# Layer 0's q, k and v: the weight columns split at k-tile 4 in place of 8, and both parts begun k-tile by k-tile in eight banks

## The reference, cut to what matters

```python
def hybrid_layer(x, c_act, g, w_ada, b_ada, w_in, w_out, dec_f, dec_b):
    mod = c_act @ w_ada + b_ada
    shift, scale, gate = jnp.split(mod, 3, axis=-1)
    h = rms_norm(x, g) * (1.0 + scale[:, None]) + shift[:, None]
    proj = jnp.einsum('bsd,df->bsf', h, w_in)
    q_a, k_a, v_a, z_a, q_r, k_r, v_r, z_r = jnp.split(proj, IN_SPLIT_IDX, axis=-1)
    ...
    y_a = dilated_attention_mixture(q_a, k_a, v_a)
    y_r = bidirectional_retention(q_r, k_r, v_r, dec_f, dec_b)
    y = jnp.concatenate([y_a * jax.nn.silu(z_a), y_r * jax.nn.silu(z_r)], axis=-1)
    return x + gate[:, None] * jnp.einsum('bsf,fd->bsd', y, w_out)
```

## Time and profile before

| | |
|---|---|
| median of 3 runs (range) | 1496.59 us (1496.10 to 1496.89) |
| profiled execution, its time | 1496.42 us |
| its span in the profile | 1494.6 us |
| mean granted TensorE clock | 0.992 |
| busy | PE 1427.5 us (96%), DVE 1169.1 (78%), ACT 722.5 (48%), POOL 117.9 (8%) |
| DMA | 448.85 MB, mean 300 GB/s |
| chain that ended last | PE 76%, DVE 14%, issue, ACT and DMA 3% each |

### The profile page before, as it was taken

How to read it: one execution, slowest core, us unless ns; L and a number is a source line. 1 busy time by engine, 2 the same in 40 slices (tenths; PEclk the granted TensorE clock), 3 DMA queues, 4 the chain that set the end, 5 groups by cost and what they waited for, 6 DMA issues and landing times.

```text
span 1494.6 us, 19097 instructions
## 1 busy us (share of the span) xinstructions
PE 1427.5 (96%) x6634; PEld 1177.8 (79%) x6634; DVE 1169.1 (78%) x1458; ACT 722.5 (48%) x1034; POOL 117.9 (8%) x217
## 2 busy tenths in 40 slices
PE   4799999999999899999999999989999999999996
PEld 3677777887887688888887878878888888888885
DVE  5999898877999799898667659878697865556566
ACT  4464554554434634444556644464345544455431
POOL 1111001001000001010010100000010000000000
PEclk9999999999999999999999999999999999999998
DMA  9999999877999599999867679759698786555762
GB/s 389 414 412 413 392 359 394 287 264 244 385 416 347 191 407 383 412 384 381 309 214 252 188 269 364 262 192 356 244 385 300 252 282 207 178 179 155 266 194 89
DMA packets 99870, 448.85 MB, mean 300 GB/s; under 512 B 11424, under 2 KB 13776, under 8 KB 76496
## 3 DMA queue, kind: packets, MB, share of 16 engines
q1 hardware_dynamic: 69840, 249.33, 46.9%
q0 software_dynamic: 26352, 185.63, 31.8%
q10 hardware_dynamic: 3600, 12.85, 2.2%
HBM read 445.65 MB, written 2.12 MB: 300 GB/s over the span
## 4 chain that ended last, share of the span: by engine, by line
PE 76%; DVE 14%; issue 3%; ACT 3%; DMA 3%; SPq 0%; POOL 0%; DVEq 0%; ACTq 0%
PE bank L741 22%; PE bank L743 22%; PE bank L742 22%; DVE gw L1425 6%; DVE w_lo L1417 4%; PE bank L951 2%; PE bank L899 2%; DMA gw<-in_t_ada 1%; PE bank L716 1%; PE bank L908 1%; DMA raw<-in_t_steps 1%; DVE area L1425 1%; ACT probs L1081 1%; PE bank L927 1%; PE bank L881 1%
## 5 line engine op out<-in xcount | busy, mean ns | idle before, releaser
L1022 ACT CAST w_hi<-raw 128x1024 fp32r<-128x1024 f32 x448 | 468.7, 1050 | 647.5 <-PE bank L743 544.4
L1405 DVE TENSOR_TENSOR w_lo<-raw,w_hi 128x1024 fp32r<-128x1024 f32 x372 | 451.4, 1223 | 260.4 <-ACT w_hi L1022 259.5
L741 PE MATMUL bank<-w_hi,act_hi 128*128 128x512 f32 x1504 | 601.3, 400 | 3.1 <-DVE w_lo L1405 3.1
L742 PE MATMUL bank<-w_lo,act_hi 128*128 128x512 f32 x1536 | 598.7, 390 | 0.0
L743 PE MATMUL bank<-w_hi,act_lo 128*128 128x512 f32 x1504 | 587.5, 391 | 0.0
L1425 DVE CUSTOM_DVE_ANT_0 gw<-gw,c_act 128x2048 f32<-128x2048 f32 x170 | 388.1, 2285 | 4.0 <-DMA gw<-in_t_ada 4.0
L742 PEld LDWEIGHTS bank<-w_lo,act_hi 128*128 128x128 f32 x1536 | 289.1, 188 | 57.2
L741 PEld LDWEIGHTS bank<-w_hi,act_hi 128*128 128x128 f32 x1504 | 282.9, 188 | 61.0 <-issue 3.6
L743 PEld LDWEIGHTS bank<-w_hi,act_lo 128*128 128x128 f32 x1504 | 282.6, 188 | 60.7
L1417 DVE TENSOR_TENSOR w_lo<-raw,w_hi 128x1024 fp32r<-128x1024 f32 x84 | 101.6, 1220 | 15.3 <-ACT w_hi L1022 15.1
L585 POOL DMA_DIRECT2D gw<-in_t_mod x96 | 51.6, 537 | 729.3 <-DVE products L1425 723.1
(11 more groups left out here) (174 smaller groups left out, 1003.3 us busy)
## 6 DMA issues: line engine op xcount, KB each, us to landing
raw<-in_t_steps SPq DMA_DIRECT2D x464, 512.0 KB, 5.7
gw<-in_t_mod POOLq DMA_DIRECT2D x96, 1024.0 KB, 7.7
gw<-in_t_ada POOLq DMA_DIRECT2D x42, 1024.0 KB, 8.3
gw<-in_t_kv_mod POOLq DMA_DIRECT2D x32, 1024.0 KB, 8.0
area<-in_t_ada POOLq DMA_DIRECT2D x6, 1024.0 KB, 10.7
area<-gate_rows ACTq DMA_DIRECT2D x3, 1024.0 KB, 12.9
area<-in_ln_g ACTq DMA_DIRECT2D x2, 1024.0 KB, 6.1
area<-in_ln_b ACTq DMA_DIRECT2D x2, 1024.0 KB, 9.2
```

The source lines that it names most:

```text
L741: nc.tensor.matmul(dst, hi, w[:, k], start=(kt == 0), stop=False)
L742: nc.tensor.matmul(dst, hi, w_lo[:, j % SLOTS, k], start=False, stop=False)
L1022: nc.scalar.copy(w_hi[:, b], raw[:, j % SLOTS]).then_inc(hi_ready, 1)
L1405: nc.vector.tensor_tensor(w_lo[:, j % SLOTS], raw[:, j % SLOTS], w_hi[:, j % LEAD].bitcast(F32), ALU.subtract).then_inc(lo_ready, 1)
```

## The change

The boundary between the two parts goes from k-tile 8 to k-tile 4 (`FIRST_KT`). Steps 0 to 7 are the eight-bank part for k-tiles 0 to 3 with chunks 0 and 2, then 3 and 4. Steps 8 to 19 give chunks 5, 8, 9, 6, 7, 1 the same four k-tiles, two steps each. Steps 20 to 43 are a second eight-bank part: k-tiles 4 to 15 one after the other for chunks 0 and 2 (banks 4 to 7) and 6 and 7 (banks 0 to 3), with the order of the two turned round at k-tile 15. Steps 44 to 79 give chunks 4, 1, 3, 5, 8, 9 the twelve k-tiles, six steps each. Rows of `w_ada` are worked one k-tile per three steps for k-tiles 4 to 7, then one per two and a half (`ROWS_AT`), the last at the same step as before. The five places for rows serve rows 0 to 9 and no longer 0 to 14. SP holds the loads to four ahead of DVE up to step 19 in place of 15. The three rows of pair 2 start at place 12 in place of 9. The small loads and the two bias tables go from behind steps 32 to 45 to behind 44 to 57, the decays, lambda and the decay tables with them by seven or eight steps. Numbers of steps, matmuls, splits and additions are the same, and the layout of the weights on the host follows the order.

```diff
-DECAYS_AT, LAMBDA_AT, C_AT = (3, 1), (3, 4), (4, 9)
-DECAY_TABLE_AT = {(3, 6): 0, (3, 8): 1, (3, 10): 2, (3, 12): 3}
+DECAYS_AT, LAMBDA_AT, C_AT = (3, 9), (3, 11), (4, 9)
+DECAY_TABLE_AT = {(3, 13): 0, (3, 15): 1, (4, 1): 2, (4, 4): 3}
...
-FIRST_ORDER = (4, 5, 8, 9, 6, 7)
-SECOND_ORDER = (6, 7, 0, 2, 4, 1, 3, 5, 8, 9)
+FIRST_KT = 4
+FIRST_WIDE = ((0, 2), (3, 4))
+FIRST_ORDER = (5, 8, 9, 6, 7, 1)
+SECOND_WIDE = ((0, 2), (6, 7))
+SECOND_ORDER = (4, 1, 3, 5, 8, 9)
+FIRST_SHORT, SECOND_SHORT = FIRST_KT // STEP_KT, (KT - FIRST_KT) // STEP_KT
+SECOND_AT = HEAD_STEPS + FIRST_SHORT * len(FIRST_ORDER)
+SHORT_AT = SECOND_AT + 2 * (KT - FIRST_KT)
+ROWS_AT = {kt: HEAD_STEPS + 3 * (kt - FIRST_KT) if kt < 2 * FIRST_KT else SECOND_AT + 5 * (kt - 2 * FIRST_KT) // 2
+           for kt in range(FIRST_KT, KT)}
+LOW_BEHIND = 4
...
-    begin, end = {2: (9, 16), 3: (0, 16), 5: (0, 15), 8: (1, 9), 18: (1, 9), 22: (0, 7)}.get(pair, (1, 14))
+    begin, end = {2: (12, 16), 3: (0, 16), 5: (0, 15), 8: (1, 9), 18: (1, 9), 22: (0, 7)}.get(pair, (1, 14))
...
+def wide_of(n):
+
+    if n < HEAD_STEPS:
+        return n // 2, FIRST_WIDE[n % 2], 4 * (n % 2)
+    kt, p = FIRST_KT + (n - SECOND_AT) // 2, (n - SECOND_AT) % 2
+
+    p = 1 - p if kt == KT - 1 else p
+    return kt, SECOND_WIDE[p], 4 * (1 - p)
...
-            return g % HEAD_RING if g < 3 * HEAD_RING else g % GEMV_RING
+            return g % HEAD_RING if g < 2 * HEAD_RING else g % GEMV_RING
...
-        SMALLS, SMALLS_AT = 12, 32
+        SMALLS, SMALLS_AT = 12, 44
...
-                if k < HEAD_STEPS:
+                if k < SECOND_AT:
 
                     wait(sp, lo_ready, k - LEAD + 1)
...
+            def wide(n):
+
+                kt, _, b = wide_of(n)
+                if n == SECOND_AT:
+                    pe.wait_ge(parted, 8)
+                if n == SECOND_AT + 1:
+                    pe.wait_ge(parted, 8 + 2 * len(FIRST_ORDER))
+                pe.wait_ge(head_hi, kt + 1)
+                pe.wait_ge(head_lo, kt + 1)
+                pe.wait_ge(lo_ready, n + 1)
...
-                q, kt0, m, j = short_of(n)
-                if j == 0 and kt0 == 0:
+                q, kt0, m, kt1 = short_of(n)
+                if kt1 == kt0 == 0:
 
                     pe.wait_ge(parted, 2 * (m + 1) if m < 2 else 8 + 2 * (m - 1))
-                elif j == 0 and m < 2:
-                    pe.wait_ge(parted, 8 + 2 * (len(FIRST_ORDER) - 1 + m))
-                elif j == 0:
-                    pe.wait_ge(evacuated, 2 * (m - 1))
+                elif kt1 == kt0:
+                    pe.wait_ge(evacuated, 2 * (m + 1) if m < 2 else 8 + 2 * (m - 1))
...
-                    kt, late = divmod(m - HEAD_STEPS, 3)
-                    if kt < HALF_KT and late < 2:
-                        gemv_step(2 * (HALF_KT + kt) + late)
-                        if late:
-                            head_finish(HALF_KT + kt)
-                    if late == 2 and 0 <= kt - 1 < HALF_KT:
-                        head_low(HALF_KT + kt - 1)
+                    for kt in range(FIRST_KT, KT):
+                        if m in (ROWS_AT[kt], ROWS_AT[kt] + 1):
+                            gemv_step(2 * kt + m - ROWS_AT[kt])
+                        if m == ROWS_AT[kt] + 1:
+                            head_finish(kt)
+                        if m == ROWS_AT[kt] + LOW_BEHIND:
+                            head_low(kt)
```

136 lines of the change are left out of this document (65 added, 71 removed).

## The result

| | before | after |
|---|---|---|
| median (range) | 1496.74 us (1496.10 to 1499.32) | 1508.39 us (1506.34 to 1510.48) |
| ratio to before (95% interval) | | 1.0072 (1.0058 to 1.0086) |
| profiled execution, its time | 1496.42 us | 1506.34 us |
| its span | 1494.6 us | 1504.4 us |
| split 39 starts, DVE | 150.09 | 156.49 |

The forecast was 1494.7 us, too near the kernel before to be told from it, with a range of 1492.6 to 1499.0 us. The measured time lies 9.4 us above the upper end. In the profiled executions the scores come 9.4 us later than before and the end 9.9 us later, so all but 0.5 us arises ahead of the scores, where the prediction looked for it. The profiled execution of the changed kernel is the fastest of its four: the profiles show 9.9 of the 11.7 us that lie between the medians.

What follows compares the result with a forecast made beforehand. DVE, with DMA right behind it, was taken to bound the front stage. The scores' gain of 3.2 - w, 1.7 us with w = 1.5, took 1496.42 to 1494.7 us; range 1492.6 to 1499.0 us.

Steps and rivals of the forecast that it cites:

- DVE's chain sets the end: Up to the first attention scores, DVE was taken as the later engine; TensorE's surplus is given back at the transposes.
- The split of step 39 ends at 149.0 + w: From 51.48 us, DVE's 97.5 us of work end with split 39 at 149.0 at the earliest, against 151.2 before.
- w: Time DVE itself waits on the way to the end of split 39: zero to 4 us, taken as 1.5.
- DMA runs dry, slower: Rival, k-tiles 5 to 7: DVE waits for vector rows, w = 7.6, time 1500.8 us; chance 12%.
- Step loads are what is late, not rows: With both queues full, step loads come 4.1 us apart; rows take 3.6 us each, less than DVE's 4.0 per row.
- Part 2: Small loads moved to steps 44 to 57: 3 us of DMA leaves the stretch before step 43, costing nothing in the new place.
- Part 3: DVE behind step 43: full from split 46 to the scores, which come at 244.6 + w, a gain of 3.2 - w.
- Split 46 at 161.0 + w: Split 46 starts when step 42 is done and 46 is cast, at 161.0 + w, against 167.64 before.
- The span of 83.6 us: Split 46 to first scores: 80.1 us before, plus one vector row (2.2 us) and one chunk addition (1.3 us).
- The wait at step 44: TensorE waits 0.8 us at step 44 for banks 0 and 1, which DVE empties only behind split 46.
- The wait at the transposes: TensorE, up to 4.5 us earlier near step 67, waits some 3 us at the first attention weights' transposes for DVE's scores.
- The rival of a lower clock: Clock falls behind small waits of steps 20 to 39; steps 39 to 42 lose 1 to 2 us: 1496; 5%.

Runs made afterwards that it cites:

- e11_loads: Changed kernel with only the hold on the step loads lifted from step 8 on, their ring of eight places kept: 1500.66 us, ratio 1.0025.
- e2_thr12: Changed kernel with step loads held to four ahead of DVE only up to step 11 in place of 19: 1507.15 us, ratio 1.0054.
- e1_ring: Changed kernel with the five row places serving rows 0 to 14 again and first-part chunks in order 5, 6, 7, 8, 9, 1: 1507.74 us, ratio 1.0064.
- e4_smalls32: Changed kernel with the small loads and bias tables back behind steps 32 to 45: 1508.10 us, ratio 1.0062.
- e13_smalls32: e11_loads with the small loads and two bias tables back behind steps 32 to 45: 1500.47 us, ratio 1.0021.
- e8_b_smalls: Kernel before with only the small loads, bias tables, decays, lambda and decay tables in their new places: 1497.78 us, ratio 1.0007.
- e9_packed: e6_early with the small loads and bias tables sent four at a time behind the loads of steps 50 to 53: 1500.24 us, ratio 1.0018.
- e16_rows2: e11_loads with pair 2's three vector rows at places 7, 8 and 12, two of them ahead of split 46: 1497.29 us, ratio 1.0000.
- e17_rows23: e16_rows2 with two of pair 3's nine rows moved ahead as well, to places 14 and 15 of pair 2: 1495.42 us, ratio 0.9986.
- e12_rows7: e11_loads with pair 2's three vector rows at places 7, 8 and 9, behind the splits of steps 43 to 45: 1503.01 us, ratio 1.0040.
- e14_rows7_packed: e12_rows7 with the small loads sent four at a time behind steps 50 to 53: 1501.74 us, ratio 1.0029.
- e18_rows23b: e17_rows23 with pair 2's five rows at places 8, 12, 13, 14 and 15, one ahead of split 46: 1498.73 us, ratio 1.0010.
- e6_early: Changed kernel with step loads from step 8 held only by their eight-place ring, and ACT's eight bank copies spread two, two, four: 1501.75 us, ratio 1.0036.

## Why the prediction was wrong, point by point

- **DVE's chain sets the end: right.** The scores' lateness is the time's (9.4 and 9.9 us), and the first transposes follow them by 4.3 us in after, e11_loads and the kernel before alike.
- **"The split of step 39 ends at 149.0 + w": the frame was right, w was the step that failed.** I took 1.5 us and allowed 4; it was 8.6 (157.6 less 149.0). My ends came from bandwidth: what DMA can move per five steps, and "1 us for the first load of the stretch". What bound was a time from request to arrival. A held load can be asked for only when DVE has done the split four before it; in the new order DVE gets from there to split 10 in 8.8 us (49.8 to 58.6), and issue to cast took 9.5. The kernel before showed 9.0 to 11.3 us for the same loads. The delay then passed through ACT's order (cast, four copies, cast) to TensorE (3.67 us at step 8) and came back to the loads: in after loads 14 to 17 went out at 61.71, 64.60, 68.50 and 72.58, each when the late split four before it was done, and in e2_thr12, without that hold, load 16 waited for step 8. The DMA engines fell to 0.81. Bandwidth did its part too: as they are full from 86 us on, the 3 MB couldn't be made good ahead of split 39. "w was 1.5" as the nearest row was taken from a stretch in which no hold was left. Lifting the hold gave 149.41 and w = 1.5, just that value.
- **The rival "DMA runs dry, slower" had the sign and the resource, not the place.** It was priced for rows (their three places, w = 7.6) and named the hold up to step 20 beside them. e1_ring and e2_thr12 show that neither is the cause by itself. My sentence "Step loads are what is late, not rows" was true, and I should have worked it out at steps 8 to 11. The rival gave 1500.8 us for a w of 7.6. The rest is a w larger by 1.0, 0.6 us at split 46, and the next point.
- **Part 2, small loads "at nothing there": wrong, the second step that failed.** The span behind split 46 took 87.0 us in place of 83.6. Moving the small loads back takes 1.5 us off it in after (e4_smalls32) and 3.0 with the hold lifted (e13_smalls32); in the kernel before the move adds 1.9 (e8_b_smalls). The cover that I named was POOL's 17.79 us without a row. It exists, and is even longer in after (23.95 us), but it didn't make them free. Why stays open: e9_packed sent all of them into that time, and the casts behind it still waited. What is shown is the price, near the 3 us that I had given for the case without cover. The gain ahead of split 46 was as forecast (2.6 to 3.7 us).
- **Part 3: right in its sums, with one thing left out.** Split 46 at 161.0 + w: 169.6 by the measured w, 170.16 found; with the hold lifted 162.6 and 163.12. The span of 83.6 us: 83.9 once the small loads are away. The wait at step 44: 0.8 forecast, 0.94 found. The wait at the transposes: about 3 forecast, 2.63 found. Left out: I counted pair 2's later rows only as 2.2 us more of DVE's work. They also hold back POOL's next loads, and e16_rows2, which moves two of the three ahead of split 46, is 3.4 us faster than e11_loads. I had also read the DMA engines of the kernel before as over 380 GB/s in slices 1 to 7; slice 6, from 187 to 224 us, is at 359.
- **The sum again with what the runs showed:** -1.7 (forecast), +7.1 (w), +0.6 (split 46), +3.4 (its span, 87.0 in place of 83.6) make +9.4 us at the scores, as measured. Even with the hold lifted the change isn't a gain: 1.0025 (1.0013 to 1.0036). How the two queues share the DMA engines, from which I took that rows come in time, no run here tests.
- **Marks that I named:** TensorE's waits for `act_lo` in the eight-bank part fell to 10.1 us, as said. Of the small waits at most steps from 22 to 39 six came, of 0.23 to 1.38 us between 133 and 158 us. Split 39 ended at 157.6 and not by 152. DVE waiting for rows between 52 and 150 us, by over 3 us, was the mark of the DMA rival. It waited 7.2 us, but 6.1 of them for casts and only 1.1 for rows.
- **The rival of a lower clock:** not found where it was looked for. The granted clock was 0.96 from 86 to 128 us, with a wait of 3.03 us at 101.75 in it, and 1.00 from 128 to 165.

What stays open: why the times of e9_packed and e17_rows23 spread over 7 to 8 us. Late executions of both were profiled, and in e17_rows23 the wait at step 44 and the low clock stand in it, but no profile of one of its early runs is there to compare.

## What to carry to other kernels

When an order is made denser, check each flow control by time and not by bandwidth: how long the consumer takes from the event that releases a load to the moment that it wants it, against what the trace shows from issue to use of that load (here 8.8 against 9.5 us). A hold that costs nothing in one order can cost more than the whole gain in another. The trace of before shows that it costs nothing there, but also the time from issue to use, and that is what the new order has to be held against. Transfers that are moved "into a gap" aren't free for that: here they gave 2.6 to 3.7 us back ahead of split 46 and took 1.5 to 3.0 behind it.

## What the hardware showed that I had not expected

- **A wait of TensorE can cost more than itself.** Granted clock behind a wait at step 44: 0.66 over 165 to 175 us after waits of 3.93, 4.29 and 5.41 us (e12_rows7, e17_rows23, e14_rows7_packed), 1.00 after waits of 2.81 and 1.11 (e16_rows2, e18_rows23b). A mean of 0.66 is a mix of the two levels, 1.2 and 2.4 GHz: in e12_rows7 one matmul follows another after 0.23 us ahead of the wait and after 0.43 us from 169.60 on. The length of the wait alone doesn't decide. In e6_early a wait of only 2.26 us at 150.88 was followed by 0.64:

```profile
150.80:155.50 4.70, 4.62 (x13) 3.69 (x14) 4.01 (x5) 1.91 (x2) 0.00 (x0) 0.64 1.02 410
```

while e11_loads, with 1.37 us there, kept 1.00 and had 21 matmul records in place of 13 in the same stretch:

```profile
150.80:155.50 4.70, 4.70 (x21) 3.87 (x22) 3.91 (x5) 2.10 (x3) 0.00 (x0) 1.00 1.01 407
```

  Split 46 comes 1.7 us later in e6_early (164.81 against 163.12). That may be why it was no better than e11_loads; I have one profile of each.
- **One late load can leave the DMA engines part empty for 28 us.** In after they moved 305 GB/s in place of 414 between 58 and 86 us, 3 MB less, and with the hold lifted 414 again (e11_loads). It took the places for rows as well: with five places in use for longer (e1_ring) the same casts were late and 387 GB/s were moved.
